# Each low part of a weight chunk is issued on GpSimd as two operations of 512 columns

## The chip, the cores and the metric

One core of a Trainium2 chip. The metric is device time in microseconds (us), the median of several runs. TensorE is PE in the profile, VectorE is DVE, ScalarE is ACT, GpSimd is POOL, and SyncE, whose queue issues the weight loads, is SP.

## What is computed

Two transformer layers in fp32 for one sequence of 512 positions and width 1024. Cut to what matters:

```python
# layer 1
h = rms_norm(x, norm_g); proj = h @ w_in            # 1024 x 3592
fox = softmax(q.k/8 + c[t] - c[s], s<=t) @ v        # 8 heads of 64
sb  = stick_breaking(q, k) @ v                      # 4 heads of 64
pool = (window means - x) @ w_pool
x = x + concat(fox, pool, sb, each gated by silu) @ w_out
# layer 2
z = rmsnorm(x) @ w_in_2
a = mla(z, positions, w_uq, w_ukv)                  # 8 heads, rope
c = short_gated_conv(z, conv_w)
x = x + rmsnorm(concat(rmsnorm(a), rmsnorm(c)) @ w_out_2)
x = x + rmsnorm((silu(h @ w_gate) * (h @ w_up)) @ w_down)   # 2816 wide
e = rmsnorm(p @ w_ple_proj)
x = x + sigmoid(x @ w_ple_gate) * e
```

## The kernel before, in words

Every large product runs on TensorE in three passes over split operands: each fp32 operand is a high part, rounded to the type fp32r, plus a low part, the rest. The helper `three` (lines 449 to 453) issues high x high (L451), high x low (L452) and low x high (L453).

The weights are laid out on the host as 142 chunks of 128 partitions x 1024 columns (512 KB). `CH[name]` is the number of the first chunk of a product; the order of the chunks is the order in which TensorE uses them. A chunk passes through three steps:

- SP loads it into `raw`, which has 2 buffers (`RAW`); load c waits until chunk c-2 is split (`w_split`).
- Its high part goes to `w_hi`, one of 4 slots (`SLOTS`), once TensorE has used the chunk that lay in that slot (`w_used`). For chunks below `SHARED` (66, the first chunk of the product "ple") GpSimd makes it (L406), from there on ScalarE does (L1049, through `weights_hi`), which tells GpSimd by `hi_shared`.
- GpSimd subtracts: `w_lo = raw - w_hi` (L411), and adds 1 to `w_split`. TensorE waits on `w_split` before it uses the chunk (`chunk`, L446).

Chunk 0 alone is split in halves of 512 columns by `split_halves` (L391 and L394), with a signal for each half.

Each engine has its own program, written out by hand in order; semaphores tie them. VectorE makes the low parts of the activations (`aT_lo`, helper `split_lo`, L1493, and helper `stt`, L1469), the residual sums (`x`, L1823), the softmax scalings (`h`, L1646), the rope rotations (L1749 to L1754), the convolution's last product before its sum of squares (L1780), the low parts of the rows staged for the down product (L1894) and the last products and sums of the output (L1935, L1937). ScalarE makes squares, exponentials and copies out of PSUM, and the high parts. Both of them share the stretches between two large products, where norms turn rows into the next left operand: there TensorE waits for them. The stretches are, in order: the norm of x and the first chunks (to 50 us), layer 1's projections (to 160), softmax and stick-breaking attention (to 285), its output product and the next norm (to 330), layer 2's projections and convolution (to 430), rope and the second attention (450 to 530), its output product, "ple" and the norm before the gated product (to 610), gate and up (to 820), down (to 955), and the last gate "pgate" with the output.

Of the kernel before, what the change touches and what calls it, by code (L numbers as in the profile page):

```python
# [8 lines left out]
F32 = mybir.dt.float32  # L9
# [3 lines left out]
ALU = mybir.AluOpType  # L13
# [162 lines left out]
def hybrid_kernel(nc, x_d, w_d, cols_d, pos_d, wpool_d, pt_d, gains_d, out_d):  # L176
    tiles = tile_counts(psum_tiles())
    with ExitStack() as ctx:
        def sb(name, shape, dt=F32):
            return ctx.enter_context(nc.sbuf_tensor(name, shape, dt))  # L180

        def sem(name):
            return ctx.enter_context(nc.semaphore(name))
# [6 lines left out]
        raw = sb("raw", [P, RAW, CW])  # L190
        w_hi = sb("w_hi", [P, SLOTS, CW], F32R)
        w_lo = sb("w_lo", [P, SLOTS, CW], F32R)
# [93 lines left out]
        hi_made, hi_shared, w_split, w_used = sem("hi_made"), sem("hi_shared"), sem("w_split"), sem("w_used")  # L286
# [46 lines left out]
        @block.sync  # L333
        def _(sp_):
            def load_x(j):
                at = slice(j * 2 * P, (j + 1) * 2 * P)
                sp_.dma_start(x[:, :, at], x_d.rearrange("(t p) c -> p t c", p=P)[:, :, at]).then_inc(x_in[j], 16)


            def load(c, first, r):  # L340
                if not first:
                    sp_.wait_ge(w_split, c - RAW + 1)
                src = w_d[bass.ds(c, 1), :, :].rearrange("a p c -> p (a c)")
                sp_.dma_start(raw[:, r, :], src).then_inc(raw_in[r], 16)

            for j in range(KD // 2):
                load_x(j)
                if j < RAW:
                    load(j, True, j)
            with sp_.Fori(1, NCH // RAW) as i:  # L350
                for r in range(RAW):
                    load(i * RAW + r, False, r)
            for n in range(2 * T):
                g, t = n // T, n % T
                sp_.wait_ge(out_made, n + 1)
                sp_.dma_start(out_d[t * P:(t + 1) * P, g * 512:(g + 1) * 512],
                              x[:, t, g * 512:(g + 1) * 512]).then_inc(out_stored, 16)
            sp_.wait_ge(out_stored, 2 * T * 16)


        @block.gpsimd
        def _(pool):
            nc.gpsimd.memset(ident[:, :], 0.0).then_inc(ident_made, 1)
            pool.wait_ge(ident_made, 1)
            nc.gpsimd.affine_select(out=ident[:, :], in_=ident[:, :], compare_op=ALU.not_equal, fill=1.0, base=0,
                                    pattern=[[-1, P]], channel_multiplier=1).then_inc(ident_made, 1)

            def masks():
                nc.gpsimd.memset(ident_b[:, :], 0.0).then_inc(masks_made, 1)
                nc.gpsimd.memset(mask_le[:, :], 0.0).then_inc(masks_made, 1)  # L370
                nc.gpsimd.memset(mask_lt[:, :], 0.0).then_inc(masks_made, 1)
                nc.gpsimd.memset(neg_tri[:, :], -1.0).then_inc(masks_made, 1)
                nc.gpsimd.memset(neg_one[:, :], -1.0).then_inc(masks_made, 1)
                nc.gpsimd.memset(ones[:, :], 1.0).then_inc(masks_made, 1)
                nc.gpsimd.memset(xp, 0.0).then_inc(masks_made, 1)
                pool.wait_ge(masks_made, 7)
                nc.gpsimd.affine_select(out=ident_b[:, :], in_=ident_b[:, :], compare_op=ALU.not_equal, fill=1.0,
                                        base=0, pattern=[[-1, P]], channel_multiplier=1).then_inc(masks_made, 1)
                nc.gpsimd.affine_select(out=mask_le[:, :], in_=mask_le[:, :], compare_op=ALU.is_ge, fill=NEG, base=0,
                                        pattern=[[-1, P]], channel_multiplier=1).then_inc(masks_made, 1)  # L380
                nc.gpsimd.affine_select(out=mask_lt[:, :], in_=mask_lt[:, :], compare_op=ALU.is_gt, fill=NEG, base=0,
                                        pattern=[[1, P]], channel_multiplier=-1).then_inc(masks_made, 1)
                nc.gpsimd.affine_select(out=neg_tri[:, :], in_=neg_tri[:, :], compare_op=ALU.is_ge, fill=0.0, base=0,
                                        pattern=[[-1, P]], channel_multiplier=1).then_inc(masks_made, 1)

            def split_halves(c, s):

                pool.wait_ge(raw_in[s], 16)
                for half in range(2):
                    at = slice(half * 512, (half + 1) * 512)  # L390
                    hi = nc.gpsimd.tensor_scalar(w_hi[:, s, at], raw[:, s, at], 1.0, 1.0, ALU.mult, ALU.mult)  # L391
                    hi.then_inc(hi_made if half else w_half, 1)
                    pool.wait_ge(hi_made if half else w_half, 1)
                    lo = nc.gpsimd.tensor_tensor(w_lo[:, s, at], raw[:, s, at], w_hi[:, s, at].bitcast(F32),  # L394
                                                 ALU.subtract)
                    lo.then_inc(w_split if half else w_half, 1)

            def split(c, s, shared, first=False):

                r = s % RAW  # L400
                if not shared:
                    pool.wait_ge(raw_in[r], (c - r) * (16 // RAW) + 16)
                    if not first:
                        pool.wait_ge(w_used, c - SLOTS + 1)
                    pool.sem_inc(slot_free, 1)
                    nc.gpsimd.tensor_scalar(w_hi[:, s, :], raw[:, r, :], 1.0, 1.0, ALU.mult,  # L406
                                            ALU.mult).then_inc(hi_made, 1)
                    pool.wait_ge(hi_made, c + 1)
                else:
                    pool.wait_ge(hi_shared, c + (1 - SHARED))  # L410
                nc.gpsimd.tensor_tensor(w_lo[:, s, :], raw[:, r, :], w_hi[:, s, :].bitcast(F32),  # L411
                                        ALU.subtract).then_inc(w_split, 1)

            def splits(a, b, shared):

                while a % SLOTS or a < SLOTS:
                    if a == 0:
                        split_halves(a, a)
                    else:
                        split(a, a % SLOTS, shared, first=(a < SLOTS))  # L420
                    a += 1
                    if a == SLOTS:
                        masks()
                with pool.Fori(a // SLOTS, b // SLOTS) as i:
                    for s in range(SLOTS):
                        split(i * SLOTS + s, s, shared)
                for c in range(b // SLOTS * SLOTS, b):
                    split(c, c % SLOTS, shared)

            splits(0, SHARED, False)  # L430
            splits(SHARED, NCH, True)
# [1608 lines left out]
```

## Time and profile before

| what | value |
|---|---|
| median of 3 runs | 1012.37 us (1009.16 to 1015.63) |
| the profiled execution | 1014.49 us |
| its span, first to last instruction | 1012.8 us |
| mean granted clock of TensorE | 0.969 of full speed |
| instructions | 12345 |
| busy share of PE, DVE, ACT, POOL | 94%, 41%, 33%, 42% |

The span is the part of the execution that the trace covers; 1.7 us lie around it. A row of the timeline gives the start in us from the span's start, the length in us, engine, line, operation, and what it writes and reads; a bracket at its end is the idle time of the engine just before, and what ended it. The length of an operation includes the time that it is held up after it has started.

### The profile page before, as it was taken

Reading aid. Unit: us, or ns where it says so; the run is one execution under the profiler, and the core shown is the slowest. Engines: PE = TensorE matmul, PEld = TensorE weight load, DVE = VectorE, ACT = ScalarE, POOL = GpSimd, SP = SyncE. Lnnn points to the kernel's source line nnn. Section 1 sums busy time; section 2 is a strip of 40 time slices with the busy share of each in tenths; the row PEclk is TensorE's granted clock in tenths of the full one; section 3 lists DMA queues with packets and bytes.
Section 4 is the critical chain, followed back from the end, with each engine's and each line's share of the span. In section 5 each row is a group of like instructions: output and inputs, shape, how many; then the busy total and the mean of one; then the engine's idle time right before and its main releaser. Section 6 shows DMA issues by size and latency. Waiting matters only on the chain.

```text
span 1012.8 us, 12345 instructions
## 1 busy us (share of the span) xinstructions
PE 947.3 (94%) x4484; PEld 756.7 (75%) x4484; DVE 413.9 (41%) x635; ACT 334.8 (33%) x659; POOL 429.1 (42%) x227
## 2 busy tenths in 40 slices
PE   7899999999997999889989599999999999998997
PEld 6689887655676988766647497888888888887785
DVE  1823474548216175654655771000000022444644
ACT  3232404445303200265543452222222232223521
POOL 7567664120055576450221345444344444443232
PEclk9899999998998999989999899999999999999999
DMA  6232321110022223211110223322323323323122
GB/s 215 83 125 86 122 86 61 42 43 1 1 68 78 84 104 104 83 62 42 42 42 22 84 83 125 104 87 99 104 84 102 104 69 119 103 83 105 42 66 101
DMA packets 26121, 82.58 MB, mean 82 GB/s; under 512 B 3920, under 2 KB 6096, under 8 KB 26080
## 3 DMA queue, kind: packets, MB, share of 16 engines
q1 hardware_dynamic: 23712, 78.65, 23.1%
q10 hardware_dynamic: 2368, 3.36, 1.1%
q8 instruction: 28, 0.46, 0.2%
q14 instruction: 13, 0.11, 0.0%
HBM read 79.87 MB, written 2.10 MB: 81 GB/s over the span
## 4 chain that ended last, share of the span: by engine, by line
PE 45%; issue 29%; POOL 14%; DVE 7%; ACT 2%; DMA 1%; POOLq 1%; SPq 0%; DVEq 0%; ACTq 0%
POOL w_lo L411 14%; PE bank L451 11%; PE bank L452 11%; PE bank L453 11%; PE bank L640 3%; PE bank L508 3%; PE bank L663 2%; PE bank L719 2%; PE bank L709 1%; PE bank L732 1%; DMA raw<-in_weights 1%; DVE h L1646 1%; ACT PT L1063 1%; DVE negmax L1639 1%; DVE h L1469 1%
## 5 line engine op out<-in xcount | busy, mean ns | idle before, releaser
L411 POOL TENSOR_TENSOR w_lo<-raw,w_hi 128x1024 fp32r<-128x1024 f32 x141 | 349.8, 2484 | 284.0 <-ACT w_hi L1049 278.5
L451 PE MATMUL bank<-w_hi,aT_hi 128*128 128x512 f32 (+4 forms) x600 | 234.7, 391 | 29.9 <-DVE aT_lo L1469 7.0
L451 PE MATMUL bank<-aT_hi,w_hi 128*128 128x512 f32 (+1 forms) x600 | 231.1, 385 | 5.2 <-DVE arena L1887 2.5
L452 PE MATMUL bank<-w_lo,aT_hi 128*128 128x512 f32 (+4 forms) x600 | 227.8, 380 | 0.0
L452 PE MATMUL bank<-aT_lo,w_hi 128*128 128x512 f32 (+1 forms) x600 | 227.5, 379 | 0.0
L453 PE MATMUL bank<-aT_hi,w_lo 128*128 128x512 f32 (+1 forms) x600 | 227.5, 379 | 0.0
L453 PE MATMUL bank<-w_hi,aT_lo 128*128 128x512 f32 (+4 forms) x600 | 227.4, 379 | 0.0
L406 POOL TENSOR_SCALAR w_hi<-raw 128x1024 fp32r<-128x1024 f32 x65 | 72.0, 1108 | 274.8 <-PE bank L453 257.9
L1049 ACT ACTIVATE w_hi<-raw 128x1024 fp32r<-128x1024 f32 x76 | 80.5, 1061 | 248.4 <-PE bank L453 231.1
L451 PEld LDWEIGHTS bank<-w_hi,aT_hi 128*128 128x128 f32 x600 | 116.3, 194 | 54.4 <-DVE aT_lo L1469 10.0
L451 PEld LDWEIGHTS bank<-aT_hi,w_hi 128*128 128x128 f32 x600 | 113.3, 189 | 26.8 <-issue 2.9
L453 PEld LDWEIGHTS bank<-w_hi,aT_lo 128*128 128x128 f32 x600 | 115.9, 193 | 20.4
L452 PEld LDWEIGHTS bank<-w_lo,aT_hi 128*128 128x128 f32 x600 | 116.7, 194 | 17.5
L453 PEld LDWEIGHTS bank<-aT_hi,w_lo 128*128 128x128 f32 x600 | 113.3, 189 | 21.2
L452 PEld LDWEIGHTS bank<-aT_lo,w_hi 128*128 128x128 f32 x600 | 113.5, 189 | 20.0 <-issue 0.2
L1887 DVE TENSOR_TENSOR arena<-arena,bank 128x512 f32 (+1 forms) x22 | 15.0, 687 | 201.0 <-PE bank L453 195.8
L1894 DVE TENSOR_TENSOR aT_lo<-arena,aT_hi 128x512 fp32r<-128x512 f32 x22 | 43.1, 1968 | 64.6 <-ACT aT_hi L1049 64.6
L508 PE MATMUL bank<-ident,h 128*128 128x128 f32 x224 | 39.5, 290 | 18.7 <-DVEq L1501 8.1
L1639 DVE TENSOR_REDUCE negmax<-bank 128x1 f32<-128x128 f32 (+1 forms) x64 | 31.3, 490 | 58.8 <-PE bank L642 57.7
L1191 ACT ACTIVATE h<-bank,negmax 128x128 f32<-128x128 f32 (+1 forms) x64 | 33.9, 530 | 61.1 <-DVE negmax L1639 61.0
L508 PEld LDWEIGHTS bank<-ident,h 128*128 128x128 f32 x224 | 26.0, 148 | 32.8 <-DVE h L1469 15.3
L640 PE MATMUL bank<-arena 66*128 66x128 f32 (+7 forms) x128 | 46.2, 441 | 0.8 <-DVE arena L1555 0.8
(174 smaller groups left out, 808.2 us busy)
## 6 DMA issues: line engine op xcount, KB each, us to landing
raw<-in_weights SPq DMA_DIRECT2D x142, 512.0 KB, 3.3
x<-in_x SPq DMA_DIRECT2D x4, 512.0 KB, 7.7
y_out<-x SPq DMA_DIRECT2D x8, 256.0 KB, 2.0
g_post<-in_gains ACTq DMA_DIRECT2D x3, 512.0 KB, 3.2
g_pre<-in_gains ACTq DMA_DIRECT2D x2, 512.0 KB, 3.7
arena<-in_pt ACTq DMA_DIRECT2D x1, 512.0 KB, 5.8
wpool<-in_wpool ACTq DMA_DIRECT2D x1, 128.0 KB, 5.8
cols<-in_cols ACTq DMA_DIRECT2D x1, 43.0 KB, 5.8
```

What stands on the lines that cost most here:

```text
L406: nc.gpsimd.tensor_scalar(w_hi[:, s, :], raw[:, r, :], 1.0, 1.0, ALU.mult, ALU.mult).then_inc(hi_made, 1)
L411: nc.gpsimd.tensor_tensor(w_lo[:, s, :], raw[:, r, :], w_hi[:, s, :].bitcast(F32), ALU.subtract).then_inc(w_split, 1)
L451: mm(out, st_hi, mv_hi, start=start, stop=False)
L452: mm(out, st_hi, mv_lo, start=False, stop=False)
L453: return mm(out, st_lo, mv_hi, start=False, stop=stop)
L508: return nc.tensor.transpose(out, in_, ident[:, :])
L640: mm(out[:, 0:kw], qT_[0:width, i, qb * P:(qb + 1) * P], kT_[0:width, i, 0:kw], start=True, stop=False)
L663: last = mm(bank[6 + pair % 2][r0:r0 + HD, kb * P:S], v_[:, kb, i * HD:(i + 1) * HD], pt_of[i % 3][:, kb, kb * P:S], start=(kb == 0), stop ...
L1049: return A(out, in_, ACT.Copy, scale=scale)
L1191: A(P_buf[:, n % 4, 0:kw], bank[n % 3][:, 0:kw], ACT.Exp, bias=negmax[:, n % 8:n % 8 + 1], accum_out=esum[:, n % 8:n % 8 + 1]).then_inc(ex ...
L1639: V.tensor_reduce(negmax[:, n % 8:n % 8 + 1], bank[n % 3][:, 0:kw], AX_X, ALU.max, negate=True)\
L1894: V.tensor_tensor(aT_lo[:, slot, :].unsqueeze(1), act[:, bass.ds(k, 1), :], aT_hi[:, slot, :].bitcast(F32).unsqueeze(1), ALU.subtract).the ...
```

## The change

The subtraction of a chunk is issued as two operations on columns 0 to 511 and 512 to 1023, one right behind the other. Only the second adds to `w_split`, so that whoever waits for the chunk still waits for all of it. `split_halves` is not touched.

```diff
--- before.py
+++ after.py
@@ -408,8 +408,11 @@
                     pool.wait_ge(hi_made, c + 1)
                 else:
                     pool.wait_ge(hi_shared, c + (1 - SHARED))
-                nc.gpsimd.tensor_tensor(w_lo[:, s, :], raw[:, r, :], w_hi[:, s, :].bitcast(F32),
-                                        ALU.subtract).then_inc(w_split, 1)
+                for half in range(2):
+                    at = slice(half * 512, (half + 1) * 512)
+                    lo = nc.gpsimd.tensor_tensor(w_lo[:, s, at], raw[:, r, at], w_hi[:, s, at].bitcast(F32),
+                                                 ALU.subtract)
+                lo.then_inc(w_split, 1)
 
             def splits(a, b, shared):
```

## Rows read from the trace of the kernel before

**Rows 1.** Page, part 1: busy us, share of the span, instructions of each engine.

```profile
PE 947.3 (94%) x4484; PEld 756.7 (75%) x4484; DVE 413.9 (41%) x635; ACT 334.8 (33%) x659; POOL 429.1 (42%) x227
```

**Rows 2.** Windows: stretch, length, busy us per engine, clock, DMA share, GB/s.

```profile
100.00:150.00 50.00, 50.00 (x233) 41.07 (x232) 30.41 (x32) 13.75 (x23) 35.31 (x20) 1.00 0.32 106
650.00:700.00 50.00, 50.00 (x222) 41.42 (x221) 2.75 (x4) 11.99 (x14) 21.51 (x9) 1.00 0.29 96
```

**Rows 3.** Groups by line, GpSimd: shapes, count, busy us, mean ns, idle before.

```profile
L411 POOL TENSOR_TENSOR w_lo<-raw,w_hi 128x1024 fp32r<-128x1024 f32 x141 | 349.8, 2484 | 284.0 <-ACT w_hi L1049 278.5
...
L406 POOL TENSOR_SCALAR w_hi<-raw 128x1024 fp32r<-128x1024 f32 x65 | 72.0, 1108 | 274.8 <-PE bank L453 257.9 <-issue 12.8 <-DMA raw<-in_weights 4.1
...
L394 POOL TENSOR_TENSOR w_lo<-raw,w_hi 128x512 fp32r<-128x512 f32 x2 | 2.5, 1270 | 0.2
```

**Rows 4.** Timeline, GpSimd and VectorE, 25 to 30 us: start us, length us.

```profile
25.91 2.38 POOL L411 TENSOR_TENSOR w_lo<-raw,w_hi 128x1024 fp32r<-128x1024 f32 x1
...
26.02 2.28 DVE L1474 TENSOR_SCALAR stat<-stat 128x4 f32<-128x4 f32 x1 [3.52 <-ACT PT L1063]
...
28.25 1.05 POOL L406 TENSOR_SCALAR w_hi<-raw 128x1024 fp32r<-128x1024 f32 x1
```

**Rows 5.** Timeline, VectorE and GpSimd, 554 to 561 us.

```profile
554.87 3.30 DVE L1823 TENSOR_TENSOR x<-x,PT 128x1024 f32<-128x1024 f32 x1
...
557.05 3.35 POOL L411 TENSOR_TENSOR w_lo<-raw,w_hi 128x1024 fp32r<-128x1024 f32 x1
```

**Rows 6.** Timeline, TensorE: first matmuls after an idle time, given in brackets.

```profile
33.62 0.79 PE L451 MATMUL bank<-w_hi,aT_hi 128*128 128x512 f32 x1 [3.99 <-DVE aT_lo L1469]
...
424.32 0.44 PE L451 MATMUL bank<-w_hi,aT_hi 128*128 128x384 f32 x1 [2.99 <-DVE aT_lo L1469]
...
489.98 0.77 PE L451 MATMUL bank<-w_hi,aT_hi 128*128 128x512 f32 x1 [1.81 <-ACT arena L1049]
...
527.08 0.91 PE L508 MATMUL bank<-ident,h 128*128 128x128 f32 x4 [1.42 <-DVE h L1646]
...
574.64 1.73 PE L508 MATMUL bank<-ident,h 128*128 128x128 f32 x7 [8.07 <-DVEq L1501]
...
611.26 0.50 PE L451 MATMUL bank<-aT_hi,w_hi 128*128 128x512 f32 x1 [2.52 <-DVE arena L1887]
...
932.90 0.50 PE L451 MATMUL bank<-w_hi,aT_hi 128*128 128x512 f32 x1 [2.82 <-DVE aT_lo L1894]
```

**Rows 7.** Timeline, VectorE: four operations beside a low part, and one without.

```profile
420.70 2.67 DVE L1780 TENSOR_TENSOR arena<-arena 128x512 f32<-128x512 f32 x1 [0.75 <-ACT arena L1260]
...
525.05 1.97 DVE L1646 TENSOR_SCALAR h<-h,erec 128x512 f32<-128x512 f32 x1
...
602.32 3.31 DVE L1469 SCALAR_TENSOR_TENSOR arena<-arena,stat,g_post 128x1024 f32<-128x1024 f32 x1
...
930.54 2.31 DVE L1894 TENSOR_TENSOR aT_lo<-arena,aT_hi 128x512 fp32r<-128x512 f32 x1 [2.79 <-ACT aT_hi L1049]
...
996.66 0.69 DVE L1935 TENSOR_TENSOR PT<-PT,arena 128x512 f32<-128x512 f32 x1 [1.82 <-ACT PT L1447]
```

**Rows 8.** Timeline, VectorE, GpSimd, TensorE, 989 to 995 us.

```profile
989.56 2.50 DVE L1935 TENSOR_TENSOR PT<-PT,arena 128x512 f32<-128x512 f32 x1 [8.23 <-ACT PT L1447]
...
991.47 2.83 POOL L411 TENSOR_TENSOR w_lo<-raw,w_hi 128x1024 fp32r<-128x1024 f32 x1
...
992.09 2.75 DVE L1937 TENSOR_TENSOR x<-x,PT 128x512 f32<-128x512 f32 x1
...
994.35 0.50 PE L451 MATMUL bank<-w_hi,aT_hi 128*128 128x512 f32 x1 [1.12 <-POOL w_lo L411]
```

**Rows 9.** Windows after and around three idle times of TensorE, columns as in rows 2.

```profile
223.60:230.40 6.80, 6.80 (x26) 2.74 (x26) 2.07 (x3) 0.02 (x1) 0.80 (x1) 0.75 0.25 77
933.50:940.30 6.80, 6.80 (x24) 5.43 (x23) 0.86 (x3) 1.49 (x5) 0.00 (x0) 0.75 0.20 75
988.00:996.00 8.00, 6.27 (x27) 4.55 (x26) 5.25 (x2) 2.58 (x3) 5.17 (x2) 1.00 0.44 156
```

## The prediction

> **What bounds the kernel now.** I read the page's busy shares first: TensorE is busy for 94% of the span, VectorE and GpSimd for 41 and 42% [rows 1]. The windows over the span say where this holds. In layer 1's projections and in the gate and up products TensorE is busy for 50.00 us out of 50 at full clock [rows 2]; the reader is to see that GpSimd is at 35.31 and 21.51 us there, so it makes chunks faster than TensorE eats them. The groups by line give GpSimd's prices: 2.48 us mean for a low part of 1024 columns, 1.11 us for a high part of 1024, and 1.27 us for a low part of 512 columns, which chunk 0 already has [rows 3]. The page's chain of waits puts 14% of the span on the low part of L411, but it walks along GpSimd's queue through stretches in which TensorE has no gap, so I don't take it for the bound. What counts is the list of TensorE's own idle times, and what ended them. Seven of the longer ones stand in [rows 6]; six end on VectorE's work and one on ScalarE's. Only near the end do the low parts themselves end a wait: 1.12 us before 994.35 [rows 8].
>
> So there are three kinds of time: dense products, where GpSimd has slack; short stretches between products, where TensorE waits for VectorE; and two or three places where TensorE waits for the low part.
>
> **How GpSimd and VectorE meet.** This is what the change touches, so the timeline of both engines side by side comes next. An operation of VectorE on 4 columns starts at 26.02, just after a low part at 25.91, and takes 2.28 us: it ends at 28.30, when the low part does (28.29) [rows 4]. So VectorE is held for the whole of the GpSimd operation. It is then done 0.01 us after the low part's end, although the next operation of GpSimd is already listed from 28.25. The other case is a long VectorE operation that waits while a second low part stands behind the first: L1823 is held from 554.87 to 558.17, and the second low part, listed from 557.05, takes 3.35 us in place of 2.38 [rows 4, 5]. The excess of 0.97 us is about the time that the VectorE operation ran. So at a boundary between two GpSimd operations the waiting VectorE operation goes first, and the second GpSimd operation stands behind it. VectorE's timeline has some 60 such holds, most beside a TensorE that never stops; [rows 7] shows four of those that matter, and a length without a neighbour.
>
> The Trainium skill has the same under "SBUF — State Buffer", in "SBUF: two separate sides": the port pair of the two engines is an exclusive lock that whoever starts first keeps for the whole instruction. By it alone the change halves the longest hold.
>
> **The change part by part.**
>
> (1) More work on GpSimd. Two halves of 1.27 us are 2.54 us against 2.38 us of an undisturbed low part, so +0.16 us for each of 141 chunks, 22 us of GpSimd time [rows 3, 4]. Even with its high part a chunk then costs 1.11 + 2.54 = 3.65 us, against the 5.4 us in which TensorE uses it (24 matmuls; 222 of them in 50 us make 0.225 us each [rows 2]). ScalarE makes the high part in the later products, which leaves still more room. Cost on the path in the dense products: nothing; TensorE hides it, and if that cover were gone it would be up to the 22 us. The first half has no signal, and nobody's wait is moved or added; w_split comes later by the 0.16 us, and SP's load of the chunk after next stands behind it, as does in turn ScalarE's high part, and the silu or sigmoid queued behind that. In the dense products each has more than a microsecond of room.
>
> (2) VectorE is held for a half and not for a whole. An operation that arrives early in a low part gets in after 1.27 us, not 2.38: up to 1.1 us earlier. If the next VectorE operation meets the second half, it is held in its turn, and the pair ends as late as before or 0.1 to 0.2 us later. So the gain exists only where one held operation is followed by something else: a read of PSUM, a hand-over to ScalarE or TensorE, or idle time. Through the idle times of [rows 6], in order:
> - 33.62: L1474 of rows 4 comes 1.1 us earlier, but the small operations behind it on VectorE meet the second half and the next high part. I take -0.9 (0 to -2.0).
> - 424.32: L1780 is held to 2.67 us where its form takes 0.69 [rows 7]; L1469, next in order, reads PSUM. Arrival 0.2 us into the low part, so I take -1.0 (0 to -1.1).
> - rope, about 435 to 444 us: two trains of small operations that all meet GpSimd. +0.2 (0 to +0.4), by the 0.16 of (1).
> - 489.98: a softmax scaling is held once, 4 us earlier, and ScalarE's copy stands between. Of the wait of 1.81 us I take a third, -0.6 (0 to -1.1).
> - 527.08: L1646 at 525.05 takes 1.97 us, and one before it is held too. -1.2 (0 to -2.5).
> - 574.64: a wait of 8.07 us behind a serial chain of norms, in which the pattern of rows 5 comes five times, each held whole operation followed by another long one. One hold shortened by 1 us survives, the rest alternate. -1.0 (0 to -2.5).
> - 611.26: four products by g_post alternate with low parts; L1469 at 602.32 takes 3.31 us. Fewer halves than wholes fall between them, -0.5 (0 to -1.0).
> - 932.90: L1894 takes 2.31 us where 0.69 would do; the next of the same line meets the second half. -0.6 (0 to -1.0).
> Together -0.9 - 1.0 + 0.2 - 0.6 - 1.2 - 1.0 - 0.5 - 0.6 = -5.6 us.
>
> (3) The low part may finish later than before, since a waiting VectorE operation now gets in between its halves. That costs where TensorE waits for the low part. At the end of the kernel the products and sums of the output, L1935 and L1937, arrive beside the last two low parts [rows 8]. Before, one of them stood between the two; now L1935 (0.69 us) slips into the first chunk and L1937 into or ahead of the second: 0.69 for the one more, and 2 x 0.16, and 0.16 for the load, the high part and the low part that led there, is 1.2 us. Nothing covers it: TensorE is dense from 994.35 to its end. I take +1.3 (0.3 to 1.7). At 557 and 560 us, where the "ple" chunks are waited for, the same gives +1.8, but the 8.07 us of idle time behind it takes that in: 0.
>
> Sum: -5.6 + 1.3 = -4.3 us. The profiled execution's 1014.49 becomes 1010.2; it lies 2.1 us above the median of 1012.37, so the median becomes 1008.
>
> (4) TensorE's clock. The windows show it at 0.75 of full over 6.80 us from 223.6 and from 933.5, so at its half level (1.2 GHz) for a part of them, the latter right behind the wait of 2.82; around 988 to 996, with 1.73 of 8 us idle, it stayed at 1.00 [rows 6, 9]. Such a stretch costs 6.80 x 0.25 = 1.7 us. Each shift of a wait may add or remove one. I take nothing, and keep two of them either way for the rivals.
>
> **The rivals.**
>
> A. No gap between the halves: GpSimd goes on into its second half before VectorE can get in. For it: in rows 4 and 5 GpSimd had semaphores to pass at the boundary, and between the two halves there are none. Against it: those semaphores had long been reached, and the listed starts overlap there as they would here. VectorE is then held for 2.54 us and not 2.38, eight places x 0.16 = 1.3, and the tail 0.3: 1014 (1012.5 to 1016). In support of A stands "GPSIMD Engine Reference" in the Trainium skill, in "Instruction dispatch": each of the eight cores starts the next instruction when it has done its own share of the last. If that keeps the ports taken, A holds; the gap seen in rows 4 and 5 speaks for a release all the same.
>
> B. The second half becomes the late one, and the end is slower than before. VectorE in the middle of a low part holds up w_split in the places of (3). Price: 1.3 at the tail, one half-clock stretch of 1.7 us there since the idle times grow to over 2 us, and 1.8 at 557 to 560 if VectorE's chain behind it turns out to wait for ScalarE: 4.8 us in all, 1017 (1015 to 1019). It decides where the savings of (2) don't reach TensorE, because ScalarE's part of those chains is next in line.
>
> C. The savings are at their upper ends, and two half-clock stretches fall away: -4.3 - 3.4 = -7.7, 1004.5 (1000 to 1005).
>
> **How the numbers follow.** The forecast has a chance of 0.50, with 1005 to 1012 as its own range; A 0.20, B 0.14, C 0.16. Forecast and C are on the faster side, A and B on the other. From 1003 to 1017 all of A and the forecast lie inside, and about half of B and of C: 0.15 is left out. About 1% (10 us) is what a measurement of this kernel can tell from no change, and the runs shown spread over 6.5 us; only the far ends of C and B cross it, with 0.04 and 0.03.
>
> **What would show it.** The groups by line must have 282 operations of L414 or thereabouts at about 1.25 us, more where VectorE intervenes. Steps (1): the dense windows stay at 50.00. (2): L1474 at 26.02 near 1.2 us, L1780 near 1.7, L1894 near 1.3, and the idle times of rows 6 shorter; under A these lengths are 2.4 and more. (3): the wait before the last dense run, 1.12 before, near 2, and a second half of over 1.8 us beside L1935. The forecast is wrong if those lengths fall and TensorE's idle times don't, or if the clock's mean leaves 0.969 by over 0.005 (5 us).

## The result, and the profile after

The change makes the kernel faster by 1.0%: 1001.31 us median of 4 runs (1000.07 to 1002.73) against 1011.26 (1009.16 to 1015.63), ratio 0.9897, 95% interval 0.9866 to 0.9927. Run again on another occasion it gave 1002.18 against 1011.00, ratio 0.9903 (0.9875 to 0.9931). The forecast was 1008, the range 1003 to 1017: the sign was right, the size less than half of it. The second measurement had been put at 8 to 12 us with a mean clock of 0.978; it gave 8.8 us by the medians and 0.977. The profiled execution took 1002.73 us, its span is 1001.0. In the experiments further down one of the twelve runs of e3 took 2394.94 us, for which nothing on record gives a reason; it is left out of e3's ratio.

The first part of the page answers to [rows 1]:

```profile
span 1001.0 us, 12486 instructions
PE 938.9 (94%) x4484; PEld 751.4 (75%) x4484; DVE 377.0 (38%) x635; ACT 334.7 (33%) x659; POOL 465.5 (47%) x368
```

Read it engine by engine. GpSimd has 141 operations more and is busy for 36.4 us more. VectorE does the same 635 operations in 36.9 us less, since an operation's length includes the time that it is held. ScalarE is as before. TensorE does the same 4484 matmuls in 8.4 us less busy time, which no shorter wait can do: its clock was higher, 0.977 on the mean and not 0.969. Of the 11.8 us that the span lost, 8.4 lie in TensorE's busy time and 3.4 in its idle time. The sum of the forecast had only the idle time.

This pair of traces makes the clock's part look larger than it is. The profiled execution of the kernel before had a low clock among its own: the mean of 65 runs of that kernel is 0.972, from 0.968 to 0.980. Runs at nearly the same clock can be compared instead. Seventeen runs of the kernel before at 0.976 have a median of 1008.1 us, and six of the change at 0.976 or 0.977 (the two measurements together) one of 1002.3. So between 5 and 6 of the 10 us are there at equal clock, and 4 to 5 us go with the clock; this split is an estimate.

The groups by line on GpSimd, for [rows 3]:

```profile
L413 POOL TENSOR_TENSOR w_lo<-raw,w_hi 128x512 fp32r<-128x512 f32 x282 | 385.7, 1390 | 248.2 <-ACT w_hi L1052 242.7
L406 POOL TENSOR_SCALAR w_hi<-raw 128x1024 fp32r<-128x1024 f32 x65 | 72.6, 1117 | 262.5 <-PE bank L456 235.1 <-issue 23.5 <-DMA raw<-in_weights 3.6
```

The dense windows, for [rows 2]. The second lies 10 us earlier than its fellow before, since TensorE has come some 8 us ahead there:

```profile
100.00:150.00 50.00, 50.00 (x251) 42.41 (x250) 25.11 (x30) 13.88 (x23) 37.87 (x30) 1.00 0.29 95
640.00:690.00 50.00, 50.00 (x222) 41.38 (x222) 2.75 (x4) 11.98 (x14) 22.81 (x18) 1.00 0.29 94
```

As forecast, TensorE is not held up by the longer GpSimd work there: 50.00 of 50 us, with GpSimd at 22.81 where it was at 21.51.

The timeline of TensorE, the matmuls after a wait, for [rows 6] in its order, with the wait for R at 49.77 put in after the first, and that for a ple chunk at 553.81. R holds the factors of the first norm, which VectorE copies out of PSUM:

```profile
31.89 0.50 PE L454 MATMUL bank<-w_hi,aT_hi 128*128 128x512 f32 x1 [1.75 <-DVE aT_lo L1472]
...
49.77 0.80 PE L454 MATMUL bank<-w_hi,aT_hi 128*128 128x512 f32 x1 [7.14 <-DVE R L1553]
...
426.25 0.66 PE L454 MATMUL bank<-w_hi,aT_hi 128*128 128x384 f32 x1 [2.44 <-ACTq L1271]
...
490.43 0.47 PE L454 MATMUL bank<-w_hi,aT_hi 128*128 128x512 f32 x1 [1.11 <-ACT arena L1052]
...
523.83 0.33 PE L511 MATMUL bank<-ident,h 128*128 128x128 f32 x1 [0.35 <-DVE h L1649]
...
553.81 0.47 PE L454 MATMUL bank<-w_hi,aT_hi 128*128 128x512 f32 x1 [1.69 <-issue]
...
566.85 0.44 PE L511 MATMUL bank<-ident,h 128*128 128x128 f32 x1 [4.35 <-DVEq L1504]
...
603.19 0.50 PE L454 MATMUL bank<-aT_hi,w_hi 128*128 128x512 f32 x1 [1.20 <-DVE arena L1890]
...
922.11 0.50 PE L454 MATMUL bank<-w_hi,aT_hi 128*128 128x512 f32 x1 [1.75 <-DVE aT_lo L1897]
```

Nearly all brackets are smaller: 3.99 is 1.75, 2.99 is 2.44, 1.81 is 1.11, 1.42 is 0.35, 8.07 is 4.35, 2.52 is 1.20 and 2.82 is 1.75. One is much larger: the wait for R, 1.03 us before, is 7.14. What came 1.7 us earlier at 33.6 is lost 15 us later, and more: at the first matmul of the attention TensorE stands at 164.14 us where it was at 160.37 before.

Where the largest saving is made, the chain of norms, VectorE's and GpSimd's timelines stand for [rows 5]:

```profile
559.73 1.87 DVE L1472 SCALAR_TENSOR_TENSOR PT<-arena,stat,g_post 128x1024 f32<-128x1024 f32 x1
561.64 2.19 DVE L1826 TENSOR_TENSOR x<-x,PT 128x1024 f32<-128x1024 f32 x1
563.76 2.28 DVE L1472 SCALAR_TENSOR_TENSOR h<-x,stat,g_pre 128x1024 f32<-128x1024 f32 x1
...
560.48 2.27 POOL L413 TENSOR_TENSOR w_lo<-raw,w_hi 128x512 fp32r<-128x512 f32 x1
...
562.72 2.24 POOL L413 TENSOR_TENSOR w_lo<-raw,w_hi 128x512 fp32r<-128x512 f32 x1
...
564.92 2.25 POOL L413 TENSOR_TENSOR w_lo<-raw,w_hi 128x512 fp32r<-128x512 f32 x1
```

The two engines alternate: each row of one starts while a row of the other runs, and each is as long as its own work and what is left of the other's. VectorE does get in between the halves, with no semaphore between them. The L1826 shown is that of the third of the four blocks of rows, which took 3.25 us before, at 569.40; the one of [rows 5], of the second block, took 3.30, of which 2.07 were its hold, and takes 2.20 now, at 550.37. The rows of the kernel before for the third block and for the wait for R:

```profile
569.40 3.25 DVE L1823 TENSOR_TENSOR x<-x,PT 128x1024 f32<-128x1024 f32 x1
...
48.01 0.50 PE L451 MATMUL bank<-w_hi,aT_hi 128*128 128x512 f32 x1 [1.03 <-DVE R L1550]
```

Rival A cited the section "Instruction dispatch" of "GPSIMD Engine Reference" in the Trainium skill; by it VectorE could have been kept out, and this trace shows that it isn't.

### The profile page after: what moved, and what is told of

Its sections match the earlier page's. It is cut to its first block, busy times and chain, and to the rows that moved or that the text cites. A ratio compares the mean times of both kernels' runs of the same rounds, so it can differ in the third digit from the quotient of the medians.

```text
span 1001.0 us, 12486 instructions
## 1 busy us (share of the span) xinstructions
PE 938.9 (94%) x4484; PEld 751.4 (75%) x4484; DVE 377.0 (38%) x635; ACT 334.7 (33%) x659; POOL 465.5 (47%) x368
## 4 chain that ended last, share of the span: by engine, by line
PE 46%; issue 25%; POOL 19%; DVE 6%; ACT 3%; DMA 1%; POOLq 0%; SPq 0%; DVEq 0%; ACTq 0%
POOL w_lo L413 19%; PE bank L454 11%; PE bank L456 11%; PE bank L455 11%; PE bank L643 3%; PE bank L511 3%; PE bank L666 2%; PE bank L722 2%; PE bank L712 1%; PE bank L735 1%; DMA raw<-in_weights 1%; ACT PT L1066 1%; DVE h L1472 1%; ACT aT_hi L1052 0%; DVE aT_lo L1496 0%
## 5 line engine op out<-in xcount | busy, mean ns | idle before, releaser
L413 POOL TENSOR_TENSOR w_lo<-raw,w_hi 128x512 fp32r<-128x512 f32 x282 | 385.7, 1390 | 248.2 <-ACT w_hi L1052 242.7
L1897 DVE TENSOR_TENSOR aT_lo<-arena,aT_hi 128x512 fp32r<-128x512 f32 x22 | 26.1, 1194 | 81.6 <-ACT aT_hi L1052 81.6
L511 PEld LDWEIGHTS bank<-ident,h 128*128 128x128 f32 x224 | 25.8, 147 | 25.9 <-DVE h L1472 11.8
```

The lines of the kernel that those rows point to most:

```text
L413: lo = nc.gpsimd.tensor_tensor(w_lo[:, s, at], raw[:, r, at], w_hi[:, s, at].bitcast(F32), ALU.subtract)
L511: return nc.tensor.transpose(out, in_, ident[:, :])
L1897: V.tensor_tensor(aT_lo[:, slot, :].unsqueeze(1), act[:, bass.ds(k, 1), :], aT_hi[:, slot, :].bitcast(F32).unsqueeze(1), ALU.subtract).the ...
```

## The experiments

Each was timed beside the kernel before. Three theories were put up. Theory 1: VectorE is held for a shorter time, each stretch gains on its own, and the clock follows the shorter waits. Theory 2: the later signals only shift the phase, and the clock falls differently by luck. Theory 3: all of it is made in the chain of norms. All kernels but e3 and e6 use this form of the change, with n chosen by chunk:

```diff
-                nc.gpsimd.tensor_tensor(w_lo[:, s, :], raw[:, r, :], w_hi[:, s, :].bitcast(F32),
-                                        ALU.subtract).then_inc(w_split, 1)
+                for part in range(n):
+                    at = slice(part * (CW // n), (part + 1) * (CW // n))
+                    lo = nc.gpsimd.tensor_tensor(w_lo[:, s, at], raw[:, r, at], w_hi[:, s, at].bitcast(F32),
+                                                 ALU.subtract)
+                lo.then_inc(w_split, 1)
```

| kernel | n | median us | before us | ratio (95%) |
|---|---|---|---|---|
| e1 | 2 below chunk 66 | 1008.67 | 1012.64 | 0.9971 (0.9951 to 0.9992) |
| e2 | 2 from chunk 66 | 1000.96 | 1012.64 | 0.9917 (0.9886 to 0.9948) |
| e3 | 64 + 960 columns | 1009.40 | 1012.64 | 0.9966 (0.9949 to 0.9983) |
| e4 | 4 | 992.47 | 1012.64 | 0.9810 (0.9784 to 0.9836) |
| e5 | 4 in chunks 66 to 75 | 1000.07 | 1012.53 | 0.9874 (0.9836 to 0.9912) |
| e6 | 1, and added matmuls | 1010.25 | 1012.53 | 0.9987 (0.9957 to 1.0018) |
| e7 | 4, but 1 in chunks 1 to 11 and the last two | 991.98 | 1012.53 | 0.9796 (0.9756 to 0.9836) |
| e8 | e7 with the added matmuls | 995.22 | 1012.53 | 0.9829 (0.9791 to 0.9868) |
| e9 | 2 in chunks 66 to 75 | 1004.86 | 1011.00 | 0.9937 (0.9909 to 0.9966) |
| e10 | 2 except in chunks 66 to 75 | 1008.95 | 1011.00 | 0.9971 (0.9949 to 0.9993) |
| e11 | the change again | 1002.18 | 1011.00 | 0.9903 (0.9875 to 0.9931) |
| e12 | e7, and 8 in chunks 66 to 75 | 992.04 | 1011.00 | 0.9808 (0.9779 to 0.9836) |

**By place: e1 and e2.** Edits: `n = 1 if shared else 2`, and `n = 2 if shared else 1`.

> Halves only in chunks below 66, where GpSimd also makes the high part; whole low parts from there on. Theory 1 (each stretch gains on its own because VectorE is held for a shorter time, and the clock follows the shorter idle times): TensorE's matmuls were 4.3 us earlier just before chunk 66 in the changed kernel's trace, so 4 us faster than before (2 to 6). Theory 2 (the later signals of GpSimd only shift the phase of things, and the clock's stretches fall differently by luck): no rule by place; the gain may be anything between 0 and 10 us, and the two partial kernels needn't add up to 10. Theory 3 (the gain is made in the chain of norms after the second attention alone): 0 to 1 us faster.

> Halves only in chunks from 66 on, whole low parts before. Theory 1: the matmuls gained 7.5 us from chunk 66 to the end, so 7 us faster than before (5 to 9), and this and the other partial kernel together give the whole change's 10 us. Theory 2: no sum. Theory 3: 9 to 10 us.

0.29% and 0.83% faster, 2.9 and 8.4 us by the ratios, together 11.3 where the whole change gives 10; by the medians it is 4.0 and 11.7. That is theory 1 within the intervals, which are wide: 0.8 to 5.0 us and 5.3 to 11.5. Theory 3 (0 to 1 us, and 9 to 10) isn't out by these two alone; e5 and e10 below decide on it.

**The same count, a long hold: e3.**

```diff
-                nc.gpsimd.tensor_tensor(w_lo[:, s, :], raw[:, r, :], w_hi[:, s, :].bitcast(F32),
-                                        ALU.subtract).then_inc(w_split, 1)
+                for at in (slice(0, 64), slice(64, CW)):
+                    lo = nc.gpsimd.tensor_tensor(w_lo[:, s, at], raw[:, r, at], w_hi[:, s, at].bitcast(F32),
+                                                 ALU.subtract)
+                lo.then_inc(w_split, 1)
```

> Two operations again, but of 64 and 960 columns: as many instructions and nearly as much GpSimd time as the change, while the longest hold of VectorE stays near 2.3 us. Theory 1: no gain, within 2 us of before. Theory 2 (what counts is that GpSimd has a second operation and signals later): the change's 10 us, at least half of it. A boundary right behind the start also lets a VectorE operation in that came early; under theory 1 that is worth at most 1 or 2 us.

It gained 0.34%, 3.4 us (1.7 to 5.2): a third of the change, where theory 2 asked for at least half. That speaks against theory 2, though the interval just reaches half; e4 and the waits of e9 and e10 speak against it more clearly. It is also more than the 2 us that theory 1 allowed. The groups by form on GpSimd, and two rows of VectorE, show why:

```profile
L412 POOL TENSOR_TENSOR w_lo<-raw,w_hi 128x960 fp32r<-128x960 f32 x141 | 328.4, 2329 | 0.0
...
L412 POOL TENSOR_TENSOR w_lo<-raw,w_hi 128x64 fp32r<-128x64 f32 x141 | 56.9, 404 | 263.9 <-ACT w_hi L1051 258.5
```

```profile
553.99 1.23 DVE L1825 TENSOR_TENSOR x<-x,PT 128x1024 f32<-128x1024 f32 x1
555.14 3.24 DVE L1471 SCALAR_TENSOR_TENSOR h<-x,stat,g_pre 128x1024 f32<-128x1024 f32 x1
```

L1825 here is of the second block of rows, the operation that took 3.30 us in [rows 5]. It came during the 64 columns and got in before the 960: 1.23 us, no hold at all. The next one is held in full, 3.24. A boundary early in the low part is worth something of its own, the length of the rest decides the remainder.

**Shorter holds: e4.** Edit: `n = 4`.

> Four operations of 256 columns. By the halves an operation costs 0.16 us beyond its columns, so a quarter takes about 0.72 us and a chunk 2.9 us. Theory 1: the longest hold falls from 1.3 to 0.7 us, half as far again as the change took it, less what more alternations cost: 2 to 4 us faster than the change, 12 to 14 us faster than before; wait times before the last dense run grow by 1 us. Theory 2: a gain without relation to the length. Rival to theory 1: trains of small VectorE operations meet four holds in place of two and the gain is lost, 0 to 3 us slower than the change.

20 us faster than before, 10 more than the change. Theory 1 had the direction, but only 2 to 4 us beyond the change; the rival is out. GpSimd's group, and the operations of the norm chain that answer to the last two of the three VectorE rows above:

```profile
L414 POOL TENSOR_TENSOR w_lo<-raw,w_hi 128x256 fp32r<-128x256 f32 x564 | 433.3, 799 | 215.9 <-ACT w_hi L1053 210.4
```

```profile
555.96 1.63 DVE L1827 TENSOR_TENSOR x<-x,PT 128x1024 f32<-128x1024 f32 x1
557.51 1.75 DVE L1473 SCALAR_TENSOR_TENSOR h<-x,stat,g_pre 128x1024 f32<-128x1024 f32 x1
```

For the x of the third block 3.25 us with whole low parts, 2.19 with halves, 1.63 with quarters: the hold is what is left of one GpSimd operation. VectorE's busy time falls to 348.3 us, and at 561 us TensorE has no wait at all:

```profile
561.00 1.04 PE L512 MATMUL bank<-ident,h 128*128 128x128 f32 x8
```

The 8.07 us are gone: this row has no bracket. The two waits for the ple chunks just before have grown in return, from 2.20 to 3.91 us together.

**Ten chunks alone: e5, e9, and the rest: e10.** Edits: `n = 4 if isinstance(c, int) and SHARED <= c < SHARED + 10 else 1` in e5, 2 for 4 in e9, and 1 there and 2 elsewhere in e10; the loop over chunks is unrolled for these ten (in e7, e8 and e12 for the first twelve too).

> Quarters of 256 columns in ten chunks only, 66 to 75, which are made beside the chain of norms between the second attention and the gate and up products; whole low parts in the other 131. Theory 1 (local gains that add up): in the trace of the kernel with quarters everywhere TensorE gained 8.2 us at the wait of 8.07 us and 2.7 us at the wait of 2.52 us, and lost 2.1 us at the ple chunks, with about 2 us of clock: 9 us faster than before (7 to 11), from ten chunks of 141. Theory 2 (luck of phase): no relation to the place, 0 to 4 us. Theory 3 (the norm chain is all of it): the whole gain of the quarters, 19 to 20 us.

> The change's halves in chunks 66 to 75 only, whole low parts in the other 131. If most of the change's gain is made in the norm chain: its trace showed TensorE 3.8 us earlier there at the wait of 8.07 us and about 1 us at the wait of 2.52 us, with clock stretches of 2 us beside them, so 6 to 7 us faster than before. If the gain lies in a little everywhere: 10 of 141 chunks give 1 us at most.

> The complement: halves everywhere except in chunks 66 to 75. If gains are local and add up, this one gives what the other lacks of the change's 10 us: 3 to 5 us faster than before. If they don't add up (a gain early is lost in a later wait): 0 to 2, or over 6.

e5: 12.5 us by the medians, above the 7 to 11, with an interval of 8.9 to 16.6. That is well short of the 19 to 20 us of theory 3, which falls. e9: 6.1 us by the medians, within what it was put up for. e10: 2.1 by the medians, 2.9 by the ratio, a little below the 3 to 5. The ratios of e9 and e10 add to 0.92%, the change timed beside them (e11) gave 0.97%: the gains are local and add up, and ten chunks of 141 make about two thirds, with intervals of 3 us to either side of e9. The waits show the same thing more sharply than the times. First e9, then e10:

```profile
567.05 0.66 PE L512 MATMUL bank<-ident,h 128*128 128x128 f32 x2 [4.39 <-DVEq L1505]
...
603.38 0.50 PE L455 MATMUL bank<-aT_hi,w_hi 128*128 128x512 f32 x1 [1.21 <-DVE arena L1891]
...
923.39 0.50 PE L455 MATMUL bank<-w_hi,aT_hi 128*128 128x512 f32 x1 [2.83 <-DVE aT_lo L1898]
```

```profile
565.57 0.45 PE L512 MATMUL bank<-ident,h 128*128 128x128 f32 x1 [8.09 <-DVEq L1505]
...
601.66 0.50 PE L455 MATMUL bank<-aT_hi,w_hi 128*128 128x512 f32 x1 [2.52 <-DVE arena L1891]
...
922.20 0.50 PE L455 MATMUL bank<-w_hi,aT_hi 128*128 128x512 f32 x1 [1.75 <-DVE aT_lo L1898]
```

With halves only there, the two waits of the norm stretch are the change's (4.35, 1.20) and the one at the down product is before's (2.82); in e10 it is the other way round.

TensorE's clock goes with these waits. The windows of 3.40 us right behind the two of them, columns as in [rows 2], again first e9, then e10:

```profile
603.40:606.80 3.40, 3.40 (x15) 2.83 (x16) 0.69 (x1) 0.65 (x2) 2.69 (x3) 1.00 0.86 251
923.40:926.80 3.40, 3.40 (x11) 2.70 (x12) 1.14 (x2) 0.00 (x0) 0.00 (x0) 0.69 0.43 154
```

```profile
601.70:605.10 3.40, 3.40 (x10) 2.69 (x11) 0.51 (x1) 1.06 (x1) 3.25 (x2) 0.61 0.70 239
922.20:925.60 3.40, 3.36 (x13) 2.48 (x14) 2.24 (x2) 0.91 (x1) 1.09 (x1) 1.00 0.34 94
```

In e9 the clock is full behind the shortened wait at the gate product and falls to its half level (1.2 GHz) for a part of the window behind the long one at the down product; in e10 again the other way round. Over all fourteen traces these two places have ten waits of 2.5 to 3.0 us, nine of them with a stretch at half level behind it (not the 2.97 us of e3), and thirteen of at most 1.75 us, none with one.

**The clock by itself: e6 and e8.** A helper puts matmuls whose results nothing reads into a bank that is free, before TensorE waits. No other work is changed, and the output is the same.

```diff
+            def fill(key, c, count, k=0, t=0):
+                bank_free(key)
+                for _ in range(count):
+                    mm(tbank(key)[:, :], left(k, t)[0], w_hi[:, c % SLOTS, 0:512], start=True, stop=True)
...
+                    if j == 3:
+                        chunk(CH["fq"] + 3)
+                        fill(("fv", 0), CH["fq"] + 3, 14)
                     left_ready(2)
...
+            chunk(CH["lq"])
+            fill(("lq", 0), CH["lq"], 22)
             turn_rows("h2", h_tile, h_made, 0, range(2, T - 1))
...
+                        if keys[t] == ("uv", T - 1):
+                            fill(("q2T", 0), CH["uv"], 20, k=2)
                         bank_free(keys[t])
...
+                if t == 1:
+                    fill(("ple", 0, 2), CH["ple"], 28, k=4, t=2)
                 if t < 2:
                     turn_rows("h3", h_tile, h_made, T, range(t, t + 1))
```

> The kernel before, with whole low parts, and 84 matmuls added whose results are overwritten unread, put into four of TensorE's waits (14 before the wait at 33.6, 22 before 324.9, 20 before 449.9, 28 before 574.6 us); they fill most of each wait. If the change's other gain came from the clock, which goes to its half level after such waits: the four stretches of 6.8 us at half that began inside those waits are gone, the mean clock rises by 0.01 or more, and the kernel is 4 to 9 us faster with not one wait for VectorE made shorter. If the clock's stretches are only a matter of chance or of the stage: clock and time as before, within 2 us.

> Both together: the added matmuls of the fill kernel and the quarters of the placed one. If waits and clock are two separate gains, more than either alone: but the waits are shorter now, so the 28 matmuls at the norm chain cost what they exceed its remaining wait (it was 0 with quarters), up to 6 us lost there; 0 to 6 us slower than the placed kernel, at a higher mean clock. If the clock is the larger part everywhere: 2 to 4 us faster than it.

Of e6's expectation the first half came true and the second didn't. The mean granted clock rose to 0.983 over 12 runs, from 0.972 over the 17 of the kernel before. But the time fell by 1.3 us only (interval 4.4 faster to 1.8 slower). By the page TensorE is busy for 956.7 us, of which 84 x 0.227 = 19 us are the added ones, so its own work takes 937.6, 9.7 us less than in [rows 1]; yet the span is only 4.3 us shorter. About 5 us are given back, most of them in two waits for VectorE that are now longer, 3.61 us for 1.03 and 2.51 for 0.42:

```profile
PE 956.7 (95%) x4568; PEld 766.3 (76%) x4568; DVE 411.9 (41%) x635; ACT 334.1 (33%) x659; POOL 428.4 (42%) x227
...
47.95 0.79 PE L451 MATMUL bank<-w_hi,aT_hi 128*128 128x512 f32 x1 [3.61 <-DVE R L1566]
...
330.24 0.58 PE L451 MATMUL bank<-w_hi,aT_hi 128*128 128x288 f32 x1 [2.51 <-DVEq L1517]
```

The windows over two of the four filled waits, first of the kernel before, then of e6, have the granted clock in the third column from the end:

```profile
31.00:40.00 9.00, 6.38 (x17) 5.02 (x18) 7.21 (x18) 2.12 (x4) 4.13 (x3) 0.62 0.34 118
571.00:580.00 9.00, 5.36 (x20) 4.60 (x21) 6.71 (x8) 4.24 (x8) 0.56 (x1) 0.62 0.18 64
```

```profile
31.00:40.00 9.00, 8.40 (x42) 6.75 (x41) 7.21 (x18) 3.23 (x5) 4.62 (x4) 1.00 0.36 119
571.00:580.00 9.00, 7.44 (x41) 6.12 (x39) 6.10 (x13) 6.25 (x12) 0.74 (x1) 1.00 0.00 0
```

So TensorE's level does depend on what it did before, and filling its waits is enough to raise it; but a faster TensorE that then waits for VectorE again is worth little. In e8 the mean clock is 0.987 and the kernel 3.2 us slower than e7. The reading that the added matmuls now exceed the waits that they fill was expected and is not shown by itself.

**The two places where the change loses: e7 and e12.** Edits: `n = 1 if isinstance(c, int) and (c < 12 or c >= NCH - 2) else 4`, and the same with 8 for chunks 66 to 75.

> Quarters everywhere except in chunks 1 to 11 and in the last two, which keep whole low parts. Theory 1: at the start the split buys nothing, since the lead of 4 us is lost in the wait for R at 48 us, whose chain of small VectorE operations is held more often; and at the end the low parts' second wait grows. Taking both back gives 2 to 5 us more than quarters everywhere: 22 to 24 us faster than before. Rival (the earlier start is worth something further on): no more than quarters everywhere, or 1 to 2 us slower than it.

> The placed kernel (whole in chunks 1 to 11 and the last two, quarters elsewhere) with eighths of 128 columns in chunks 66 to 75. The wait of 8.07 us was gone with quarters, so a shorter hold has little left to give there; each eighth costs another 0.16 us of GpSimd and the ple chunks come 0.6 us later: within 2 us of the placed kernel, 19 to 22 us faster than before. Rival: VectorE is still held at 0.7 us a time in the chain, so 2 to 4 us more.

e7's waits answer as theory 1 says: for R 1.96 us and not 7.38 as in e4, for the last but one low part 0.73 and not 2.23 (for the last 1.22 where e4 has 1.09). Its time doesn't: 991.98 against 992.47, where 2 to 5 us were expected. Of the 5.4 us that the wait for R is shorter, 3.0 are there because TensorE starts later, at 33.82 and not 30.80 behind a wait of 3.30 us where quarters have 0.95. Another 1.6 are there because it then runs in part at half level; it leaves the wait for R only 0.8 us earlier. e12 is as expected, nothing beyond e7; quarters had already emptied the norm chain. The best of these are e4, e7 and e12, which the runs can't tell apart, all about 2% faster than before.

## Why the prediction was wrong

The mechanism was right: the dense products hide the 0.16 us per chunk, VectorE gets in at the boundary, its holds are halved, and the low parts are late only at the ple chunks and at the end. Two steps failed: step (2) had the holds of long operations too small and left out the wait for R, and step (4) took nothing for the clock. The errors within step (2) cancel: the waits that it went through, with those for the ple chunks counted in, fell by 11.1 us where it took 5.6, and the wait for R grew by 6.1. That the idle time as a whole, 3.4 us less, comes near the 4.3 of the sum is luck. What puts the time outside the range is then step (4).

The term of step (2) at 574.64 us, "-1.0 (0 to -2.5)", is the first that was mis-sized. It rested on the sentence that with halves the holds "alternate", so that one hold shortened by 1 us survives. It measured 3.7 us at that wait (8.07 to 4.35). Of these, 1.3 only take in the later ple chunks, as step (3) had said, and 0.4 of idle time between fell away too, so 2.9 us are left for this term, still outside the bounds. Before, four long operations of VectorE were held for about 2 us each there; after, it was five, for 0.6 to 1.0 us each. I had let each half find a waiting VectorE operation, but a long one (1.2 to 1.3 us of its own) takes as long as a half, and there are not enough of them: the number of holds went from 4 to 5, not to 8. The same sort of error stands at 611.26 (-0.5, measured -1.3), at 527.08 with its neighbours (-1.2, measured -2.2) and at 932.90 (-0.6, measured -1.1). e9 shows the norm stretch as a whole at 6 us.

Step (4), "I take nothing", is the second and larger. TensorE's busy time fell by 8.4 us in the trace through the higher clock; over the runs the mean went from 0.972 (25 runs of before) to 0.978 in the change's first four runs and 0.977 in the next six; by the estimate above that is worth 4 to 5 us. The prediction's own sign of being wrong, a mean that leaves 0.969 by over 0.005, came in. Rival C had the clock with the right sign at two stretches of 1.7 us, and at 0.16 it was held too unlikely: shorter waits don't only shift the half-level stretches, they take some away, as behind 611.26 and 932.90. e9 and e10 show this by place, and e6 shows the dependence by itself. Not every stretch follows a wait of the change: the one at 223.6 of [rows 9] is gone too, behind waits that are as before (0.82 and 0.69 us).

The signs that it named for steps (1) to (3) came in or nearly: L1477 on 4 columns takes 1.00 us (1.2 was said), L1783 1.59 (1.7), L1897 1.25 (1.3), a second half beside L1938 1.71 (over 1.8); a low part's half has a mean of 1.39 us (1.25). One reading was wrong, without weight in the sum: low parts end a wait not only near the end, but for 1.63 us at 560.45 too.

Right or nearly so: 489.98 (-0.6, measured -0.7), 424.32 (-1.0, measured -0.55, since ScalarE came next), rope (+0.2, -0.15), the tail of step (3) (+1.3; the two waits there are 1.65 + 1.24 = 2.89 us and were 0.61 + 1.12 = 1.73, so +1.2):

```profile
979.66 0.50 PE L454 MATMUL bank<-w_hi,aT_hi 128*128 128x512 f32 x1 [1.65 <-POOL w_lo L413]
...
982.58 0.50 PE L454 MATMUL bank<-w_hi,aT_hi 128*128 128x512 f32 x1 [1.24 <-POOL w_lo L413]
```

and the +1.8 at the ple chunks, covered by the wait behind them (+1.3 there, 1.69 + 1.77 us where 0.57 + 1.63 stood).

Not foreseen was the wait for R. The -0.9 at 33.62 was -2.2 by its bracket, but the chain of small operations behind it on VectorE, which makes the rope angles and then R, meets GpSimd more often than before:

```profile
32.45 1.08 DVE L1537 TENSOR_SCALAR cs<-cols,pos_f 128x16 f32<-128x16 f32 x1
33.56 1.34 DVE L1537 TENSOR_SCALAR cs<-cols,pos_f 128x16 f32<-128x16 f32 x1
...
34.94 1.21 DVE L1537 TENSOR_SCALAR cs<-cols,pos_f 128x16 f32<-128x16 f32 x1
...
45.52 3.47 DVE L1550 MEMSET arena<- 2x4096 f32 x1 [0.80 <-issue]
49.02 0.69 DVE L1553 COPY R<-bank 128x512 f32<-128x512 f32 x1
```

Each of the first three works for a quarter of a microsecond and is held for the rest, by a high part and both halves of a low part. Two more are held a little later (1.00 us at 37.92, 1.31 at 38.96), by the next chunk; before, the whole chain met a single low part. Here, with short operations in a train, more boundaries do mean more holds, as step (2) said for rope: R is ready 1.8 us later (49.71, before 47.95). That is only a part of the 6.1 us by which the wait grew. Another 1.7 are there because TensorE starts 1.7 us earlier, and 2.6 because its matmuls between the two waits ran at full clock, where before they ran in part at half. The delay of R itself isn't the same in every execution: it comes again in e11 (49.72), but in e10, whose first 65 chunks are split alike, the two later holds are missing and R is ready at 47.65. So "one hold per boundary" describes these trains of short operations and is wrong for long ones; I had used it for both.

Of the rivals, A is refuted: VectorE enters between two halves. B's lateness is real (1.2 us at the end), but no half-level stretch came with it, and it decides nothing. C comes nearest: the measured 1001.31 lies in its range of 1000 to 1005. Its own sum is 1012.37 - 7.7 = 1004.7, not 1004.5, and it adds the clock to the forecast's -4.3, not to savings at their upper ends as its text says.

## What to carry to other kernels

Where GpSimd and VectorE meet, look at VectorE's operations that are longer than their form needs, and ask which of them TensorE or ScalarE waits for; here cutting the GpSimd work into shorter operations cost 0.16 us each and freed VectorE at each boundary, which paid beside long VectorE operations and not beside trains of short ones. Ten of 141 chunks gave two thirds of this gain, and quarters twice that of halves, so cut fine at the places where somebody waits. And when a change shortens waits of TensorE, count the clock with it, but only so far as TensorE doesn't run into its next wait.

## What the runs showed of the hardware

A VectorE operation with no semaphore to wait for gets in between two GpSimd operations that stand one right behind the other, also with none between them: 2.19 us for L1826 with halves, 1.63 with quarters, 1.23 when it arrives during a first operation of 64 columns. Operations with a single input from SBUF are held as well: one of 128x16 took 1.34 us where 0.23 is usual, and one of 128x4 took 2.28 in [rows 4] and 1.00 with halves. An operation of 64 columns has a mean of 0.40 us on GpSimd and one of 256 of 0.80, both with some time behind VectorE in them, and one of 960 has 2.33.

That 84 matmuls with no use raised the mean granted clock from 0.972 to 0.983, and left the time nearly as it was, was not expected: it had been put at 4 to 9 us. Why the clock's gain in the change itself was not given back in the same way is shown only in part: its waits behind the half-level stretches became shorter at the same time, while in e6 they didn't. How much of the clock's part would remain without the shorter holds was not measured.
